# The expert stage of a two-layer diffusion backbone: from a loop over groups of experts to a straight program with neighbouring experts interleaved

## The reference, cut to what matters

```python
def expert_choice_ffn(h, w_router, w1, w3, w2):
    cap = EC_FACTOR * n // N_EXPERTS                      # 32 tokens for each expert
    aff = jax.nn.softmax((h @ w_router).astype(jnp.float32), axis=-1)
    g, idx = lax.top_k(jnp.swapaxes(aff, 1, 2), cap)
    xs = h[bidx, idx]
    hid = jax.nn.silu(jnp.einsum('becd,edf->becf', xs, w1)) * jnp.einsum('becd,edf->becf', xs, w3)
    y = jnp.einsum('becf,efd->becd', hid, w2) * g[..., None].astype(h.dtype)
    return jnp.zeros_like(h).at[bidx, idx].add(y)

for l in range(DEPTH):
    ...
    x = x + gt2 * rmsnorm(expert_choice_ffn(h2, w_router[l], w_e1[l], w_e3[l], w_e2[l]), g_post2[l])
    if ctx_out:
        ...
        xc = xc + gtc2 * rmsnorm(expert_choice_ffn(hc2, w_router[l], w_e1[l], w_e3[l], w_e2[l]), g_post2[l])
```

## Time and profile before

| | us |
|---|---|
| median of 3 runs | 2058.98 |
| lowest and highest run | 2053.08, 2063.93 |
| the profiled execution's own time | 2061.82 |
| its span, first to last instruction | 2060.0 |
| mean granted TensorE clock (share of full speed) | 0.92 |

### The profile page before, as it was taken

The page is one execution under the profiler, slowest core; times in us unless marked ns, Lnnn a source line. Parts: engine busy times, 40 slices in busy tenths (PEclk is TensorE's granted clock), DMA queues, the critical chain, the costliest instruction groups (busy, mean ns, idle before and its releaser), DMA issues.

```text
span 2060.0 us, 22838 instructions
## 1 busy us (share of the span) xinstructions
PE 1750.1 (85%) x9237; PEld 885.5 (43%) x9237; DVE 468.6 (23%) x972; ACT 317.6 (15%) x742; POOL 93.0 (5%) x162
## 2 busy tenths in 40 slices
PE   5999999999998978889788799999995677676775
PEld 2656454444475323233232266857883232232321
DVE  1144044211114112121021422344114010010102
ACT  2113244100024000000000321243011000000001
POOL 4000110000003000000000000110001000000000
PEclk9999999999999999999999999999996686686867
DMA  9210104545317998999989941105633999999996
GB/s 349 90 42 21 16 1 184 195 153 204 123 62 261 371 421 354 422 388 395 422 360 421 410 151 54 36 1 173 195 125 137 421 421 422 422 422 422 422 422 278
DMA packets 130632, 524.62 MB, mean 255 GB/s; under 512 B 9886, under 2 KB 73532, under 8 KB 75276
## 3 DMA queue, kind: packets, MB, share of 16 engines
q1 hardware_dynamic: 127884, 520.47, 64.0%
q0 software_dynamic: 2688, 3.32, 0.9%
HBM read 522.70 MB, written 1.05 MB: 254 GB/s over the span
## 4 chain that ended last, share of the span: by engine, by line
PE 59%; DMA 33%; DVE 5%; ACT 2%; issue 1%; SPq 0%; DVEq 0%; ACTq 0%
DMA ring<-in_w_e_dram 31%; PE ps L649 13%; PE ps L897 9%; PE ps L1015 7%; PE ps L903 4%; PE ps L933 4%; PE ps L1033 3%; PE ps L861 3%; PE ps L589 2%; PE ps L823 2%; PE ps L992 2%; PE ps L1050 2%; PE ps L739 2%; DMA ring<-in_w_mod_dram 1%; PE ps L595 1%
## 5 line engine op out<-in xcount | busy, mean ns | idle before, releaser
L1015 PE MATMUL ps<-ring,arena 128*32 128x256 f32 (+1 forms) x3072 | 424.1, 540 | 124.8 <-DMA ring<-in_w_e_dram 121.4
L1015 PEld LDWEIGHTS ps<-ring,arena 128*32 128x32 f32 (+1 forms) x3072 | 135.3, 136 | 403.8 <-DMA ring<-in_w_e_dram 244.8
L1033 PE MATMUL ps<-ring,arena 128*32 128x256 f32 (+1 forms) x1536 | 212.8, 548 | 53.4 <-DMA ring<-in_w_e_dram 34.8
L897 PE MATMUL ps<-arena,ring 128*128 128x512 f32 (+1 forms) x576 | 192.4, 487 | 0.0
L649 PE MATMUL ps<-arena,ring 128*128 128x512 f32 (+1 forms) x480 | 176.9, 527 | 1.4 <-DVE arena L1479 1.4
L1067 ACT ACTIVATE arena<-ps 128x256 f32<-128x256 f32 (+4 forms) x144 | 71.8, 500 | 538.7 <-PE ps L589 368.1
L1033 PEld LDWEIGHTS ps<-ring,arena 128*32 128x32 f32 (+1 forms) x1536 | 69.1, 138 | 181.8 <-DMA ring<-in_w_e_dram 78.3
L897 PEld LDWEIGHTS ps<-arena,ring 128*128 128x128 f32 x576 | 108.7, 190 | 77.9 <-issue 70.4
L1645 DVE COPY arena<-ps 32x512 f32<-32x512 f32 (+1 forms) x128 | 70.9, 554 | 293.1 <-PE ps L1033 291.8
L1640 DVE TENSOR_TENSOR arena<-arena,ps 128x512 f32<-128x512 f32 (+1 forms) x32 | 17.7, 555 | 487.2 <-PE ps L1015 487.2
L649 PEld LDWEIGHTS ps<-arena,ring 128*128 128x128 f32 x480 | 90.8, 191 | 83.6 <-issue 77.7
(11 more groups left out here) (186 smaller groups left out, 1303.1 us busy)
## 6 DMA issues: line engine op xcount, KB each, us to landing
ring<-in_w_e_dram SPq DMA_DIRECT2D x384, 1024.0 KB, 17.7
ring<-in_w_mod_dram SPq DMA_DIRECT2D x48, 1024.0 KB, 9.3
ring<-in_w_in_dram SPq DMA_DIRECT2D x44, 1024.0 KB, 10.3
ring<-in_w_out_dram SPq DMA_DIRECT2D x8, 1024.0 KB, 9.9
arena<-in_w_br_ml_dram SPq DMA_DIRECT2D x8, 512.0 KB, 6.3
arena<-in_w_br_mla_dram SPq DMA_DIRECT2D x8, 256.0 KB, 3.9
arena<-in_w_br_na_dram SPq DMA_DIRECT2D x8, 256.0 KB, 4.6
arena<-in_rpb_dram POOLq DMA_DIRECT2D x16, 96.0 KB, 4.1
```

Source lines behind the costliest of these rows:

```text
L897: mm = pe.matmul(ps[:, u % 3, tq], wg[:, k, cols], hT[:, k, tq], start=k == 0, stop=k == KD - 1)
L1015: mm = pe.matmul(ps[M * j:M * j + M, b0 + m, 0:NW], XST[:, kk, e, 0:M], w[:, k, j * NW:(j + 1) * NW], start=kk == 0, stop=kk == KD - 1)
L1033: mm = pe.matmul(ps[M * j:M * j + M, 6 + e % 2, 0:NW], lhs, w[:, k, j * NW:(j + 1) * NW], start=kk == 0, stop=kk == KD - 1)
```

## The change

The loops become straight programs. The ring's loads run in a new order: w1 and w3 of expert e, then w2 of expert e - 1. TensorE's program for step e is: w1 of e, transposes of e - 1's `hid`, one piece of group work, w3 of e, w2 of e - 1. The pieces of group work are: the scatter of the group before in the second expert of a group, the gather of the next group in the third, the transposes of the gates in the fourth. `XST` is held twice. PSUM is dealt out anew: banks 0, 1, 2 and 3 for w1, w3, the transposes and w2 of every expert, banks 4 to 7 for gather, gates and scatter. The gates are transposed straight out of `Sg`; GpSimd's copies in the loop go. The first gather waits for `Ssel` of all streams. Several tiles get other places in the arena. The diff, cut to its core:

```diff
-EXP_LOADS = 12
-LOOP_LOADS = GROUP * EXP_LOADS
-LOOPS = N_EXP // GROUP
+GROUPS = N_EXP // GROUP
+EXPERT_LOADS = []
+for _e in range(N_EXP + 1):
+    if _e < N_EXP:
+        EXPERT_LOADS += [(_e, m, q) for m in range(2) for q in range(4)]
+    if _e:
+        EXPERT_LOADS += [(_e - 1, 2, q) for q in range(4)]
...
-        junk1 = view(21056, D)
+        junk1 = view(10240, D)
...
-        XST = view(8192, KD, GROUP, 64)
-        stg = view(10240, 2, 2, P)
+        XST = [view(8192 + 2048 * b, KD, GROUP, 64) for b in range(2)]
...
-                with sp.Fori(0, LOOPS) as i:
-                    for e in range(GROUP):
-                        for m, w in enumerate((w_e1, w_e3, w_e2)):
...
-                                sp.wait_ge(used, i * LOOP_LOADS + (n - SLOTS + 1))
-                                sp.dma_start(w_slot(n), we[bass.ds(i, 1), e, q].rearrange("i p m -> p (i m)"))\
-                                  .then_inc(landed[n % SLOTS], 16)
+                for e, m, q in EXPERT_LOADS:
+                    w = (w_e1, w_e3, w_e2)[m][l, e].rearrange("(q p k) n -> q p (k n)", q=4, p=P)
+                    load(n, w_slot(n), w[q])
+                    n += 1
...
-                with pool.Fori(0, LOOPS) as i:
-
-                    pool.wait_ge(sem("gathered"), before("gathered", l) + i * (2 * L.ns) + 1)
-                    for si in range(L.ns):
-                        for c2 in range(2):
-                            ins = pool.tensor_copy(stg[:, si, c2, :], Sg[:, si, c2, bass.ds(i * P, P)])
-                    ins.then_inc(sem("staged"), 1)
+                pool.nop().then_inc(sem("weighted"), 1)
...
+                def gather(g):
+
+                    if g >= 2:
+                        pe.wait_ge(sem("ya_added"), before("ya_added", l) + 1 + NB_ * (g - 1))
...
+                def turn_gates(g):
+
+                    if g == 0:
+                        pe.wait_ge(sem("weighted"), before("weighted", l) + 1)
+                    last = 2 * min(g + 2, GROUPS)
+                    pe.wait_ge(sem("xs_lat"), before("xs_lat", l) + last)
...
+                def scatter(g):
+
+                    pe.wait_ge(sem("y_taken"), before("y_taken", l) + (g + 1) * GROUP)
+                    pe.wait_ge(sem("gt_ready"), before("gt_ready", l) + g + 1)
+                    pe.wait_ge(sem("ya_added"), before("ya_added", l) + 1 + NB_ * g)
...
+                def expert_in(e, m):
...
+                        w = next_slot().rearrange("p (k n) -> p k n", k=2)
+                        if q == 0 and e:
+                            if m == 0:
+                                pe.wait_ge(sem("silu"), before("silu", l) + e)
+                            else:
+                                pe.wait_ge(sem("hid_ready"), before("hid_ready", l) + e)
...
+                pe.wait_ge(sem("ya_added"), before("ya_added", l) + 1)
+                pe.wait_ge(sem("routed"), before("routed", l) + 2 * L.ns)
+                gather(0)
+                for e in range(N_EXP + 1):
+                    if e < N_EXP:
+                        expert_in(e, 0)
+                    if e:
+                        turn_units(e - 1)
+                    g, at = divmod(e, GROUP)
+                    if at == 1 and g:
+                        scatter(g - 1)
+                    if at == 2 and g + 1 < GROUPS:
+                        gather(g + 1)
+                    if at == 3:
+                        turn_gates(g)
+                    if e < N_EXP:
+                        expert_in(e, 1)
+                    if e:
+                        expert_out(e - 1)
+                scatter(GROUPS - 1)
```

More of the change, by code:

```diff
@@ L300, in backbone @@
         h2T = view(8192, KD, T)
[L301 to L308 removed]
+        XST = [view(8192 + 2048 * b, KD, GROUP, 64) for b in range(2)]
+        Yg = view(12288, 2, D)
+        Ya = view(14336, 4, D)
+        sgh = view(18432, 512)
+        hid = view(18944, 512)
+        hidT = view(19456, 512)
+        G2 = view(19968, 2, D)
         tmp2 = view(9216, D)
         junk2 = view(8192, D)
[L311 to L318, removed]
+        aff = view(22016, 4, N_EXP)
+        lg = view(22080, 4, N_EXP)
+        affT = view(22144, SEQ)
+        lgT = view(22400, T)
+        wk = [view(22400 + 256 * b, SEQ) for b in range(2)]
+        GT = view(22400, 2, SEQ)
+        msk = view(22912, SEQ)
+        csum = view(23168, SEQ)
+        pmT = view(23424, 2, 32)
         ps = stack.enter_context(nc.psum_tensor("ps", [P, 8, 512], F32))
@@ new lines, in turn_gates @@
+                def turn_gates(g):
[3 more added lines that the diff above has]
+                    pe.wait_ge(sem("xs_lat"), before("xs_lat", l) + last)
+                    if L.ns == 2:
+                        pe.wait_ge(sem("xs_ctx"), before("xs_ctx", l) + last)
+                    for si in range(L.ns):
+                        for c2 in range(2):
+                            mm = transpose(ps[:, 4, (2 * si + c2) * P:(2 * si + c2 + 1) * P],
+                                           Sg[:, si, c2, g * P:(g + 1) * P], P)
+                    mm.then_inc(sem("gt_tr"), 1)
@@ new lines, in turn_units, with expert_out @@
+                def turn_units(e):
+                    pe.wait_ge(sem("hid_ready"), before("hid_ready", l) + e + 1)
+                    for b in range(nb):
+                        mm = transpose(ps[:, 2, b * P:(b + 1) * P], hid[:, paired(b)], P)
+                    mm.then_inc(sem("hid_tr"), 1)
+                def expert_out(e):
+                    pe.wait_ge(sem("hidT_ready"), before("hidT_ready", l) + e + 1)
+                    if e:
+                        pe.wait_ge(sem("y_taken"), before("y_taken", l) + e)
+                    for q in range(4):
+                        w = next_slot().rearrange("p (k n) -> p k n", k=2)
+                        for k in range(2):
+                            kk = 2 * q + k
+                            lhs = hidT[:, (kk % nb) * P + (kk // nb) * M:(kk % nb) * P + (kk // nb) * M + M]
+                            for j in range(NT):
+                                mm = pe.matmul(ps[M * j:M * j + M, 3, 0:NW], lhs,
+                                               w[:, k, j * NW:(j + 1) * NW], start=kk == 0, stop=kk == KD - 1)
+                        mm.then_inc(used, 1)
@@ new lines, in _ @@
+                if L.ns == 2:
+                    gathered_ctx(0)
+                for e in range(N_EXP + 1):
+                    if e < N_EXP:
+                        act.wait_ge(used, expert_load(l, e, 0, 3) + 1)
+                        if e:
+                            act.wait_ge(sem("hid_ready"), before("hid_ready", l) + e)
+                        act.activation(sgh[:, 0:NW], ps[:, 0, 0:NW], ACT.Silu).then_inc(sem("silu"), 1)
+                    if e:
+                        act.wait_ge(sem("hid_tr"), before("hid_tr", l) + e)
+                        copy(hidT[:, 0:NW], ps[:, 2, 0:NW]).then_inc(sem("hidT_ready"), 1)
+                    g, at = divmod(e, GROUP)
+                    if at == 2 and g + 1 < GROUPS and L.ns == 2:
+                        gathered_ctx(g + 1)
+                    if at == 3:
+                        act.wait_ge(sem("gt_tr"), before("gt_tr", l) + g + 1)
+                        copy(GT[:, 0:L.ns, :], ps[:, 4, 0:256 * L.ns].rearrange("p (s t) -> p s t", s=L.ns))\
+                            .then_inc(sem("gt_ready"), 1)
```

185 lines of the change are left out of this document (74 added, 111 removed).

## The result

| | before | after |
|---|---|---|
| median of the runs taken together, us | 2057.26 (5 runs, 2053.08 to 2063.93) | 2042.77 (5 runs, 2040.65 to 2043.30) |
| ratio after / before | | 0.9928, 95% interval 0.9912 to 0.9944 |
| the profiled execution's own time, its span | 2061.82, 2060.0 | 2042.77, 2041.0 |

The changed kernel is 14.5 us faster, 0.7%; 21 were forecast.

The account below looks back on a forecast made before the run. DMA landing of expert weights was taken as the bound, with pauses in layer 0: 2061.8 - 23.4 + 1.3 + 1.0 = 2040.7 us profiled, 2038 for the median; 8-in-10 range 2031 to 2050, the forecast's own 2033 to 2045.

Parts of the forecast that it names:

- the case that was called likeliest: Whole kernel: the full gain within its bounds, 2038 us for the median, own range 2033 to 2045; chance 0.73.
- What bounds the kernel: Expert stages: DMA limits at 422 GB/s; layer 0 loses 23.4 us below full rate, layer 1 has nothing to be had.
- Scatter and gather apart, -23.4: Layer 0's group turns: parting scatter and gather keeps the DMA at full rate, saving 23.4 us, bounds 0 and 23.8.
- the two views, 23.4 and 23.8: Layer 0's three turns: time lost by the rate windows, 23.4 us, and by the spacing of groups, 23.8 us.
- The working of the cover: Layer 0: loads under way, landing 17.7 us after issue, outlast pauses of 10.1 and 8.2 us; ring never dry.
- Rival A: Layer 0: pauses outlast the loads under way and restart loss stays; 2050 us with half the gain gone; chance 0.15.
- First gather, +1.3: Layer 0's first gather waits for two more VectorE operations on `Ssel`: 1.3 us more, bounds 0 and +3.
- Straight code, +1.0: Stages the DMA limits: unrolled code adds 0.42 MB of instructions to fetch, 1.0 us at 422 GB/s.
- the claim that it had nothing to give: Layer 1's expert stage already runs at full DMA rate, so its length stays as before within 2 us.
- Rival C: TensorE's queue in layer 1: code arrives too late and holds TensorE, +40 us, 2078 us; chance 0.07.
- Everything else at nothing: Load order, added waits, result copies, bank and arena layout, and each layer's tail: booked at no time.
- The clock, rival B: Layer 0's experts: TensorE's clock falls to 0.67 as in layer 1, giving 2178 us; chance 0.05.

Follow-up runs that it names:

- the copy with more code: Changed kernel with 450 empty GpSimd instructions, each adding to a semaphore, beside each of 15 experts of layer 1: 2115.83 us, ratio 1.0272.
- that experiment: Changed kernel with the next group's gather moved from the third to the second expert, right behind the scatter: 2053.21 us, ratio 0.9963.
- Three straight programs in other orders: Straight code: kernel before unrolled in old order, 2061.91 us; changed kernel with gather right behind scatter, 2053.21 us; changed with each expert's loads in own order, 2042.79 us.

## Why the prediction came out as it did

The time, 2042.77, lay 4.8 above the forecast and within its range, and in the case that was called likeliest. The gain is a weaker hit: 14.5 us where 21 were forecast, 6.5 short, of which 1.7 don't show in the time, because the kernel before came out that much faster in these runs than in the three that the forecast was shifted to. That part is luck. By its steps, with stages as means of the profiles at hand (before: layer 0 490.5 over five, layer 1 465.7 over the four with the loop kept; after, its copy with bare empty instructions and, for layer 0, the copy with more code: 471.1 and 470.0):

- **What bounds the kernel: right.** The DMA's rate in layer 0 was the thing to look at, and it now stands at 421.
- **Scatter and gather apart, -23.4: right in kind, 4.0 too large.** 19.4 us over all profiles, 21.1 in the pair first compared. The three turns themselves gave 22.3 there (381.7 to 359.3), and 1.2 came back at the two ends of the stage, which the sum didn't look at; 421 instead of the 422 GB/s of the sum are 1.1 us of 470. 0.8 is the choice of one profile, whose layer 0 was longer than the mean (the two views, 23.4 and 23.8, were both of it). And 1.55 us, in part the same as the missing GB/s, are the late load behind a piece of code: straight code has a price in layer 0 too. The working of the cover held for pauses of 7.5 and 7.8 us, shorter than the 10.1 and 8.2 that it assumed; taken to the end it was too generous, as the two pauses of 15.7 us, still below the 17.7 of a landing, lost 3.5 us each. Rival A, the cover too thin, is what that experiment shows, not the change.
- **First gather, +1.3: 0.5.** It starts later, as said, but runs 9.80 us instead of the 10.36 of the earlier trace rows, the catching up that was the lower bound:

```profile
660.15 2.51 DVE arena L1666 x4
662.79 9.80 PE ps L991 x64
```

- **Straight code, +1.0: the step that failed.** "1.0 is the row's bytes": the bytes were foreseen (0.42 MB, 26 pieces; measured 0.51 and 31), the price wasn't. Layer 1 takes 4.2 us more, against the claim that it had nothing to give and would stay within 2 us. Three straight programs in other orders show the same (470.2, 470.3, 469.1), the loop fetched once doesn't (465.1). My row for the price, the first turn of layer 0's loop, came from a stage in which the DMA had pauses for it. Rival C had the right place and the wrong form: TensorE hardly waits for code (3.1 us put down to issue in all), the weights come late: three loads, each behind a piece of code, 3.75 us together. The third of them is the last load of the stage. It takes 19.87 us beside 17.86, and the last product waits for it:

```profile
1983.99 17.86 DMA ring<-in_w_e_dram
...
2003.02 19.87 DMA ring<-in_w_e_dram
...
2022.94 1.98 PE ps L1060 x16
```

  In the packet records a piece of code is a single packet of 16 KB that takes about 1.07 us, where a weight packet takes 0.31. A load is complete when its last packet is, so one delayed packet may delay a whole load. That late loads follow pieces of code is shown by the records; that this is the road, and why seven of eight pieces cost nothing, is not shown.
- **Everything else at nothing: right**, with one exception of no weight: the last step of a layer has no next w1 to cover the copies of the expert before, and TensorE waits 1.3 us for them in layer 1 (the last row of the waits above).
- **The clock, rival B: did not happen.** Layer 0's windows show 1.00, with TensorE waiting for most of its loads.

Together -19.4 + 0.5 + 4.2 = -14.7 us, beside -14.5 between the medians; as the stretch between the stages alone varies by some us from run to run, so close an agreement is partly chance.

The best version is the changed kernel with layer 1 left as a loop, at a place where the loop is kept: 2036.74 us. It and the changed kernel were each timed against the kernel before (0.9900 and 0.9928, intervals that overlap slightly), not against each other; the 4.9 us between their stages in layer 1 say which of the two is better, and why.

## What to carry to other kernels

Where the DMA bounds a stage, ask of each pause of the consumer whether the loads under way outlast it, with room for the restart: here pauses of 7.5 us cost nothing, one of 15.7 us cost 3.5 and one of 20.0 cost 7.8. Moving scatter and gather apart, out of the place where they also waited for other engines, gave the gain; removing the waits inside the experts gave none. Unroll only where it pays: straight code has to come in beside the weights, and a stage that already ran at full rate lost 4.2 us by it. And when any edit ahead of a long loop changes the time of the loop, look at the number of code pieces and at waits put down to issue at its turn before explaining it by the edit.

## What was not expected of the hardware

- A loop of some 1,700 TensorE instructions takes 465 or 484 us for the same work depending on its place: moved by 168 instructions, it cost 18 us of stage and 16 us of median, more than this whole change gained. The kernel before happened to lie well.
- GpSimd's code comes over another queue (q14) in pieces of 8 KB; 47 of them beside full-rate loads went with 24.4 us in the stage, about 0.7 us late for each load that one held up.
- Of the 16 KB pieces that come over q8 beside full-rate loads, the same three, eight apart, each held up one load of layer 1 by 1.0 to 1.5 us in five programs; the others there held up none by more than 0.4 us.
- Bare empty instructions don't reach the chip's program; with a semaphore update they do.
